# Moving one subtraction of the stick-breaking attention from the vector engine to GpSimd, and computing its scores with two stacked products instead of three

## What is computed

```
z = einsum('bqhd,bkhd->bhqk', qb, kb) * scale
mask = s_idx[None, :] < t_idx[:, None]
log_fail = where(mask, log_sigmoid(-z), 0.0)
after = cumsum(log_fail, axis=3, reverse=True) - log_fail
log_a = log_sigmoid(z) + after
a = where(mask, exp(log_a), 0.0)
out = einsum('bhqk,bkhd->bqhd', a, vb)
```

## Time and profile before

| | |
|---|---|
| times of three runs | 2904.34, 2911.0, 2911.57 us |
| the profiled execution: its own time | 2908.29 us |
| its span, from first to last instruction | 2906.5 us |
| PE busy | 2839.6 us (98%), 12826 instructions |
| DVE busy | 1793.6 us (62%) |
| ACT busy | 1019.7 us (35%) |
| POOL busy | 1006.3 us (35%) |
| TensorE clock granted, mean | 0.994 of full |
| stick stage, first to last score product | 189.7 to 365.0 us |

### The profile page before, as it was taken

The page is one execution under the profiler, slowest core; times in us unless marked ns, Lnnn a source line. Parts: engine busy times, 40 slices in busy tenths (PEclk is TensorE's granted clock), DMA queues, the critical chain, the costliest instruction groups (busy, mean ns, idle before and its releaser), DMA issues. The chain is left out here.

```text
span 2906.5 us, 32794 instructions
## 1 busy us (share of the span) xinstructions
PE 2839.6 (98%) x12826; PEld 2250.9 (77%) x12826; DVE 1793.6 (62%) x1884; ACT 1019.7 (35%) x1492; POOL 1006.3 (35%) x595
## 2 busy tenths in 40 slices
PE   8999999999999999999999999999999899999998
PEld 7876677787878888778888866776887778888876
DVE  4649954877765555883332175565538787777557
ACT  3148943566530101441002143334015455552012
POOL 2320023265543332243333330300344545553334
PEclk9999999999999999999999999999999999999999
DMA  3131032355662322321323343431341222214232
GB/s 122 51 80 30 1 138 96 136 187 206 230 217 87 116 87 95 117 103 51 116 73 129 108 113 126 109 73 48 136 150 51 87 87 80 87 74 151 88 114 88
DMA packets 111042, 308.12 MB, mean 106 GB/s; under 512 B 21744, under 2 KB 31216, under 8 KB 110128
## 3 DMA queue, kind: packets, MB, share of 16 engines
q1 hardware_dynamic: 105168, 285.40, 29.1%
q10 hardware_dynamic: 5728, 20.74, 1.8%
HBM read 212.96 MB, written 64.75 MB: 96 GB/s over the span
## 5 line engine op out<-in xcount | busy, mean ns | idle before, releaser
L327 POOL TENSOR_SCALAR w_hi<-w_raw 128x1024 fp32r<-128x1024 f32 x116 | 127.0, 1095 | 1185.3 <-PE ps L1905 229.8
L329 POOL TENSOR_TENSOR w_lo<-w_raw,w_hi 128x1024 fp32r<-128x1024 f32 x116 | 304.3, 2623 | 9.7
L420 PE MATMUL ps<-x_hi,w_hi 128*128 128x512 f32 x656 | 203.8, 392 | 0.1
L420 PE MATMUL ps<-x_lo,w_hi 128*128 128x512 f32 x656 | 202.1, 389 | 0.0
L420 PE MATMUL ps<-x_hi,w_lo 128*128 128x512 f32 x656 | 201.9, 389 | 0.0
L2036 DVE TENSOR_TENSOR down_sums<-down_sums,ps 128x1024 f32<-128x1024 f32 x112 | 132.7, 1217 | 68.2 <-PE ps L1905 68.2
L3783 POOL TENSOR_TENSOR op_low<-op_sum,op_high 128x512 fp32r<-128x512 f32 x84 | 111.1, 1334 | 150.4 <-DVE op_sum L3777 104.3
L1905 PE MATMUL ps<-hidden_hi,w_hi 128*128 128x512 f32 x480 | 147.9, 389 | 2.1 <-DVE down_sums L2036 2.1
L1905 PE MATMUL ps<-hidden_lo,w_hi 128*128 128x512 f32 x480 | 147.8, 389 | 0.0
L1905 PE MATMUL ps<-hidden_hi,w_lo 128*128 128x512 f32 x480 | 147.8, 389 | 0.0
L420 PEld LDWEIGHTS ps<-x_hi,w_hi 128*128 128x128 f32 x656 | 122.7, 188 | 27.3 <-issue 1.9
(11 more groups left out here) (573 smaller groups left out, 7603.2 us busy)
## 6 DMA issues: line engine op xcount, KB each, us to landing
w_raw<-wall SPq DMA_DIRECT2D x140, 512.0 KB, 3.8
ada_raw<-wada SPq DMA_DIRECT2D x48, 512.0 KB, 5.5
pair_raw<-wall SPq DMA_DIRECT2D x44, 512.0 KB, 4.1
hidden_scratch<-up_out SPq DMA_DIRECT2D x32, 512.0 KB, 9.0
hidden<-hidden_scratch SPq DMA_DIRECT2D x32, 512.0 KB, 4.5
up_raw<-wall SPq DMA_DIRECT2D x28, 512.0 KB, 6.9
residual<-residual_scratch SPq DMA_DIRECT2D x24, 512.0 KB, 7.1
hidden_scratch<-conv_out SPq DMA_DIRECT2D x22, 512.0 KB, 2.6
```

The costliest lines, as they stand in the source:

```text
L327: nc.gpsimd.tensor_scalar(w_hi[:, slot, :], w_raw[:, slot, :], 1.0, 1.0, ALU.mult, ALU.mult).then_inc(w_split, 1)
L329: nc.gpsimd.tensor_tensor(w_lo[:, slot, :], w_raw[:, slot, :], w_hi[:, slot, :].bitcast(F32), ALU.subtract).then_inc(w_split, 1)
L420: last = nc.tensor.matmul(ps[:, banks + c, :], lhs, x[:, k0 + k, c * HALF:(c + 1) * HALF], start=k == 0 and n == 0, stop=k == nk - 1 and n ...
```

## The change

Four things change together.

1. `low` moves from DVE to POOL, into `stick_gpsimd`, one per step. `softplus` now also waits for the low part of three steps before (the ring `stick_sp` has three places), and `low` for the two sums of four steps before.
2. Scores in two passes' worth of columns: the low keys times the high queries for both heads at once (as before, the third product), and then for each head by itself one product over 128 rows, whose upper 64 rows are the high queries and whose lower 64 rows the low queries of that head (`q_twice`), against the head's high keys written twice (`k_twice`). Columns per wide step: 512 + 256 + 256 instead of 3 x 512; in a narrow one 256 + 128 + 128 instead of 3 x 256.
3. SP copies for that: `spread_q` issues 6 DMAs a pair instead of 4, the new `double_k` 4 more, `clear_q` 2 instead of 4. DVE zeroes one tile in place of two.
4. The written order: scores and exp run one step further ahead (i+4), ln, softplus and high too (i+3). On PE `sum_later` works on step i (it was i+1) and comes before `sum_block`. On ACT the exp now stands ahead of the copy, and the probability of a narrow step comes one iteration earlier.

```diff
@@ spread_q, double_k (SP)
-        for src, dst in zip((q1_hi, q1_lo), q_wide[p % 2]):
-            for h in range(2):
-                r = slice(h * HD, (h + 1) * HD)
-                sp.dma_start(dst[r, :, h, :].bitcast(F32), src[r, p, :].bitcast(F32).rearrange("q (c n) -> q c n", c=4)
-                             ).then_inc(q_spread.sem, 16)
+        for h in range(2):
+            r = slice(h * HD, (h + 1) * HD)
+            for src, dst, to in ((q1_hi, q_wide, h), (q1_hi, q_twice, 0), (q1_lo, q_twice, 1)):
+                sp.dma_start(dst[p % 2][to * HD:(to + 1) * HD, :, h, :].bitcast(F32),
+                             src[r, p, :].bitcast(F32).rearrange("q (c n) -> q c n", c=4)).then_inc(q_spread.sem, 16)
+
+    def double_k(sp, p):
+        for h in range(2):
+            for n in range(2):
+                sp.dma_start(k_twice[p][h][n * HD:(n + 1) * HD, :].bitcast(F32),
+                             k1_hi[h * HD:(h + 1) * HD, p, :].bitcast(F32)).then_inc(q_spread.sem, 16)
...
@@ front_sync (SP)
             if b == 16:
-                sp.wait_ge(*q_zeroed.at(2))
+                sp.wait_ge(*q_zeroed.at(1))
                 spread_q(sp, 0)
+            if b == 18:
+                sp.wait_ge(w_used, 14 + 3)
+                double_k(sp, 0)
...
@@ stick_gpsimd (POOL)
-        pool.wait_ge(*spl_done.at(NS))
+        def low(k):
+            pool.wait_ge(*sph_done.at(k + 1))
+            if k >= 4:
+                pool.wait_ge(*c_full.at(k - 3))
+                pool.wait_ge(*t_done.at(sums_to(k - 4)))
+            nc.gpsimd.tensor_tensor(at(spl, k), at(sp_buf, k), at(sph, k).bitcast(F32), ALU.subtract
+                                    ).then_inc(spl_done.sem, 1)
+
+        for k in range(NS):
+            low(k)
         split_blocks(pool, GO + 1, GO + 2)
...
@@ stick_scalar (ACT)
-        for i in range(-3, NS + 1):
-            if 2 <= i + 2 < NS:
-                stick_log(act, i + 2)
-            if i >= 1:
+        for i in range(-4, NS + 1):
+            if 2 <= i + 3 < NS:
+                stick_log(act, i + 3)
+            if i >= 1 and not first_of_chunk(i - 1):
                 probability(i - 1)
+            if 0 <= i < NS and first_of_chunk(i):
+                probability(i)
+            if 2 <= i + 4 < NS:
+                stick_exp(act, i + 4)
             if 0 <= i < NS:
                 copy_later(i)
-            if 2 <= i + 3 < NS:
-                stick_exp(act, i + 3)
...
@@ stick_vector (DVE)
             dve.wait_ge(*l_done.at(k + 1))
+            dve.wait_ge(*spl_done.at(k - 2))
...
-        def low(k):
-            dve.wait_ge(*sph_done.at(k + 1))
-            nc.vector.tensor_tensor(at(spl, k), at(sp_buf, k), at(sph, k).bitcast(F32), ALU.subtract
-                                    ).then_inc(spl_done.sem, 1)
...
-        for i in range(-2, NS + 3):
+        for i in range(-3, NS + 3):
             if 0 <= i < NS:
                 add_later(i)
-            if 0 <= i + 2 < NS:
-                softplus(i + 2)
-                high(i + 2)
-                low(i + 2)
+            if 0 <= i + 3 < NS:
+                softplus(i + 3)
+                high(i + 3)
...
@@ stick_scores (PE)
-        for n, (a, b) in enumerate(((k1_hi, q_hi2), (k1_hi, q_lo2), (k1_lo, q_hi2))):
-            last = nc.tensor.matmul(z_bank(k)[:, :, columns(k)], a[:, p, ks], b[:, c, :, columns(k)],
-                                    start=n == 0, stop=n == 2, skip_group_check=True)
...
+        last = nc.tensor.matmul(z_bank(k)[:, :, columns(k)], k1_lo[:, p, ks], q_wide[p % 2][:, c, :, columns(k)],
+                                start=True, stop=False, skip_group_check=True)
...
+        for h in range(2):
+            last = nc.tensor.matmul(z_bank(k)[:, h, columns(k)], k_twice[p][h][:, ks],
+                                    q_twice[p % 2][:, c, h, columns(k)], start=False, stop=h == 1, skip_group_check=True)
...
@@ stick_tensor (PE)
-        for i in range(-3, NS + 2):
-            if 2 <= i + 3 < NS:
-                stick_scores(pe, i + 3)
+        for i in range(-4, NS + 2):
+            if 2 <= i + 4 < NS:
+                stick_scores(pe, i + 4)
+            if 0 <= i < NS:
+                sum_later(i)
             if 0 <= i + 1 < NS:
                 sum_block(i + 1)
...
-            if 0 <= i + 1 < NS:
-                sum_later(i + 1)
```

More of the change, by code:

```diff
@@ L659, in _program @@
     k1_hi, k1_lo = slots("stick_k_hi", 36, 4, F32R), slots("stick_k_lo", 28, 4, F32R)
-    q_wide = [tuple(slots(f"stick_q_{part}_{n}", first + 2 * i, 2, F32R, [P, 4, 2, STICK_Q])
-                    for i, part in enumerate(("hi", "lo"))) for n, first in enumerate((32, 12))]
+    q_wide = [slots(f"stick_q_wide_{n}", first, 2, F32R, [P, 4, 2, STICK_Q]) for n, first in enumerate((32, 12))]
+    q_twice = [slots(f"stick_q_both_{n}", first, 2, F32R, [P, 4, 2, STICK_Q]) for n, first in enumerate((34, 14))]
+    k_36 = slots("stick_k_twice_36", 36, 1, F32R)[:, 0, :]
+    k_twice = [(temp("stick_k_twice_t", 4, 1, F32R)[:, 0, :], slots("stick_k_twice_11", 11, 1, F32R)[:, 0, :]),
+               (k_36, slots("stick_k_twice_24", 24, 1, F32R)[:, 0, :]),
+               (slots("stick_k_twice_37", 37, 1, F32R)[:, 0, :], slots("stick_k_twice_25", 25, 1, F32R)[:, 0, :]),
+               (slots("stick_k_twice_38", 38, 1, F32R)[:, 0, :], k_36)]
     y_pool = slots("pool_out", 20, 4)
@@ L941, in front_vector @@
         dve.wait_ge(w_used, 12 + 3)
-        for t in q_wide[0]:
-            nc.vector.memset(t[:, :, :, :].bitcast(F32), 0.0).then_inc(q_zeroed.sem, 1)
+        nc.vector.memset(q_wide[0][:, :, :, :].bitcast(F32), 0.0).then_inc(q_zeroed.sem, 1)
     FRONT = ((square_ready, 8), (square_added, 8), (stat_full, 2), (rstd_ready, 4),
@@ L957, in _program @@
     t_sb = stick_ring("stick_later", 3, 7)
-    a_buf = stick_ring("stick_a", 4, 12)
-    sph = stick_ring("stick_sp_hi", 4, 16, F32R)
-    spl = stick_ring("stick_sp_lo", 4, 20, F32R)
+    sph = stick_ring("stick_sp_hi", 4, 10, F32R)
+    a_buf = stick_ring("stick_a", 4, 14)
+    spl = stick_ring("stick_sp_lo", 4, 18, F32R)
     o1 = slots("stick_o", 16, 4)
@@ L1006, in clear_q @@
     def clear_q(sp):
[L1008 to L1011, removed]
+        for h in range(2):
+            r = slice((1 - h) * HD, (2 - h) * HD)
+            sp.dma_start(q_wide[1][r, :, h, :].bitcast(F32), q_wide[0][r, :, h, :].bitcast(F32)).then_inc(q_cleared.sem, 16)
     def stick_sync(sp):
@@ L1018, in stick_sync @@
                 sp.wait_ge(*z_full.at(last_of_pair(p - 2)))
-                sp.wait_ge(*q_spread.at(64 * p))
+            sp.wait_ge(*q_spread.at(160 * p))
             spread_q(sp, p)
+            double_k(sp, p)
         load_blocks(sp, GO + 3, GO + 4)
-        sp.wait_ge(*q_spread.at(256))
+        sp.wait_ge(*q_spread.at(640))
     def stick_gpsimd(pool):
-        pool.wait_ge(*spl_done.at(NS))
+        def low(k):
[7 more added lines that the diff above has]
+            low(k)
         split_blocks(pool, GO + 1, GO + 2)
@@ L1088, in high @@
             dve.wait_ge(*sp_done.at(k + 1))
[L1089 to L1093, removed]
+            if k >= 5:
+                dve.wait_ge(*c_full.at(k - 4))
+                dve.wait_ge(*t_done.at(sums_to(k - 5)))
             nc.vector.tensor_copy(at(sph, k), at(sp_buf, k)).then_inc(sph_done.sem, 1)
-        def low(k):
-            dve.wait_ge(*sph_done.at(k + 1))
-            nc.vector.tensor_tensor(at(spl, k), at(sp_buf, k), at(sph, k).bitcast(F32), ALU.subtract
-                                    ).then_inc(spl_done.sem, 1)
         def add_later(k):
@@ L1149, in stick_scores @@
         pe.wait_ge(*freed(k - Z_RING))
-        for n, (a, b) in enumerate(((k1_hi, q_hi2), (k1_hi, q_lo2), (k1_lo, q_hi2))):
-            last = nc.tensor.matmul(z_bank(k)[:, :, columns(k)], a[:, p, ks], b[:, c, :, columns(k)],
-                                    start=n == 0, stop=n == 2, skip_group_check=True)
[L1153 to L1157, removed]
+        last = nc.tensor.matmul(z_bank(k)[:, :, columns(k)], k1_lo[:, p, ks], q_wide[p % 2][:, c, :, columns(k)],
+                                start=True, stop=False, skip_group_check=True)
+        if j >= 2 * c:
+            cs = columns(k).start
+            nc.tensor.matmul(z_bank(k)[:, :, cs:cs + P], ident[:, :],
+                             mask[:, :].unsqueeze(1).to_broadcast([P, 2, P]),
+                             start=False, stop=False, skip_group_check=True)
+        for h in range(2):
+            last = nc.tensor.matmul(z_bank(k)[:, h, columns(k)], k_twice[p][h][:, ks],
+                                    q_twice[p % 2][:, c, h, columns(k)], start=False, stop=h == 1, skip_group_check=True)
         last.then_inc(z_full.sem, 1)
```

11 lines of the change are left out of this document (5 added, 6 removed).

## The result

| | before | after |
|---|---|---|
| median (lowest to highest), us | 2909.64 (2904.34 to 2911.57) | 2885.86 (2884.17 to 2888.35) |
| profiled execution, us | 2908.29 | 2884.95 |
| span, us | 2906.5 | 2883.2 |
| stick stage, first exp behind the front stage to last probability, us | 175.3 | 155.3 |

The ratio is 0.9921, 95% interval 0.9907 to 0.9934: 23 us less (19 to 27). Between the two profiled executions the span fell by 23.3 us, and the stage gave 20.0 of them. In what follows "stage" is always this stretch, read from the one profiled execution of a kernel.

The account below looks back on a forecast made before the run. DVE was taken as the bound; afterwards ACT's 146 us, about 1.3 at the end and 9 of waits make a 156.3 us stage, a gain of 19, so 2891 us in all, range 2882 to 2905.

Parts of the forecast that it names:

- The bound before is DVE: Stick stage: DVE, busy 169.6 of 176 us, makes the others wait; moving the low part takes 44.6 us off it.
- The sum: Stick stage: ACT's 146 us, about 1.3 at the end and 9 of waits make 156.3, a gain of 19.
- GpSimd at 1.3 us: Low part on POOL: 1.3 us per instruction, one a step, so POOL idles at 2.0 us a step.
- Scores: Score products on PE: 0.22 us saved per wide step, 64 times, 14 us; narrow steps taken as 0.
- PE level with ACT: Middle of the stick stage: PE within 1% of ACT, 4.00 against 4.04 us for two wide steps.
- The copy between exp and ln: ACT's turn: a copy between exp and its ln saves 0.14 us per pair, 79 pairs, 11.1 us, less 2.2.
- The DMAs: SP copies for the stage: 10 a set instead of 4, there in time; cost 0, or 4 us if late.
- The last score product: Sign in the profile after: PE's last score product of the stage near 347 us in place of 365.0.
- The lock: DVE's rounding can't start while POOL works: 1.83 us loop, no loss; POOL at 1.69 gives about 2902 us; chance 0.10.
- The slower rival: Rounding and POOL's low part loop, POOL at 2.28 us: stage 205, total 2941; decides from 1.9 us; chance 0.07.
- the order: Stick stage: running one step further ahead covers POOL's low part; ACT's copies follow `sum_later` with 0.0 to 0.6 us spare.
- no change: Stick stage: a step's chain over five banks, not engine load, sets the pace; time within 9 us; chance 0.07.

Follow-up runs that it names:

- GpSimd longer: Changed kernel with GpSimd computing the first half of each wide low part twice, an additional 128x256 subtraction with its own wait: stage 165.3 us, ratio 0.9961.

## Why the prediction was right, point by point

- *The bound before is DVE; relieve it and the gain comes.* Shown: with the low part on DVE the stage is 174.4, 0.9 us shorter than before.
- *The sum, 156.3 us of stage, a gain of 19, 2889 to 2892 in all (2891 said, range 2882 to 2905).* Measured 155.3, 20.0 and 2885.86. Inside the stage two terms were off and cancelled in part: ACT was busy 148.3 us where 146 stood, and idle 7.0 where 9 of waits and 1.3 at the end stood. On the profiled execution, 2889.3 was forecast and 2884.95 measured, 4.3 us less: 1.0 in the stage; 1.2 ahead of it, which is scatter (the first exp is at 189.6 to 191.0 us in all profiles, and differs as much between kernels with the same front stage); and 2.1 behind it, where I had said that all is shifted as a whole. 1.2 of these 2.1 lie right behind the stage. GpSimd's weight split ran at 371.03 to 373.40 beside DVE's first y_lo subtraction before, which took 3.23 us; after, it ran at 348.60 to 350.98 and ended 0.9 us after DVE had begun, so that this one took 1.98. The other three took 1.21 in both. This is read from two traces, not tested; the remaining 0.9 is less than two executions differ by in the later stages.
- *GpSimd at 1.3 us.* 1.27 to 1.31 in every wide step. The slower rows came from the last MLP: there all 61 of the kind with a median of 1.69 overlapped a DVE instruction that reads SBUF alone, while of the other kind the 53 that met no such instruction took 1.31 at most.
- *Scores.* 0.22 us less in a wide step, as said; 0.07 less in a narrow one, where I took 0 (bounds 0 to 0.12).
- *PE level with ACT.* Shown for PE: with 14 us more of scores PE is busy 142.6 of 144 us and the stage is 161.4. For ACT it rests on its idle time, 5.3 us of 196 to 346, and on the copy ahead of the exp, where more work on ACT lengthened the stage; the run with less on ACT brought late copies with it and settles nothing.
- *The copy between exp and ln.* 9 us expected (0.14 in 64 steps), 7.9 measured, but only 42 wide steps had the pair to lose (5.9 us); the rest is idle time and in part the clock.
- *The DMAs.* No wait for them: `double_k` was issued from 175.50 to 178.94, and in the stage no row of the waits of PE, DVE, ACT or GpSimd names SP or a DMA.
- *The last score product, said to be near 347.* It was at 340.9, mainly since the scores also run one step further ahead: from the last score product to the last probability there were 6.3 us before and 9.3 after.
- *The lock.* The rounding does stand still while GpSimd works, as the Trainium skill, "SBUF — State Buffer", section "SBUF: two separate sides", has it: ten of the 64 wide ones were lengthened, by 3 us together. That it costs nothing was right. The slower rival was to decide from 1.9 us of GpSimd work a step. At 2.1 us a step, in two instructions, the stage is still 165.3, 10 us better than before, since the rounding comes in between the two; what a single instruction of that length would do was not run.

Where the argument was weak is *the order*. The prediction said that running ahead covers GpSimd's 1.3 us and that `sum_later` and the copies have 0.0 to 0.6 us to spare, and counted some waits for it. It priced no part of the order beyond the exp and ln, and gave 0.07 to the rival "no change", dismissed because a step's latencies add up to 7 us where five banks leave 11 (to fill them they would have to be 1.6 times as long, not twice). The runs show that this sum does not decide. Each engine takes its list in order, so one early need behind one late delivery in a turn stops it. With all of the order missing the stage is 17.6 us longer, with the depth or the sequence alone 17.7 and 17.5; with the narrow probability alone put back it is 21.4 longer, with `sum_later` alone 24.6. With any of these the change would have gained 2.5 us of the stage at most or lost up to 4.6, with the profile before looking just the same.

These prices do not add up. Only the new depth is the narrow probability, `sum_later` and the copy all put back, and it costs 17.7 us where they cost 21.4, 24.6 and 7.9 one by one (with the highest estimate for the clock taken off, 16.0 where they cost 16.3, 16.1 and 4.5). A placement is good or bad only together with the others; why the three together cost no more than one was not followed up.

That the forecast held was in part luck. I had followed the new sequence for the middle of a chunk (the 0.0 to 0.6 us), but for its ends, where the narrow probability stands, not at all. Even the changed kernel is not free of this wait: PE's scores stand behind the narrow probability in 15 places for 10.5 us, in the waits above. It does not seem to cost the stage much, since ACT idled only 7.0 us in it; one turn later the same wait is 31.9 us.

## What to carry to other kernels

When a stage is bound by one engine, add up start-to-start times of every engine for one turn of the loop: the gain ends at the next of these sums, whatever the first engine is relieved of (20 us here, of 44.6 taken off DVE). Then walk through one turn of each in-order list, and at the ends of the loop too, and ask for every wait what the engine delivering it has to do before: here each of two single placements was worth as much as the whole gain, and a third a part of it. Test such placements together as well as one by one, since their costs did not add up. Moving work onto an idle engine lengthens the path it lies on (0.69 to 1.29 us); here it needed a step more of depth, and the depth brought up the next thing that frees a buffer. And look at PE's clock before a stage time is put down to the order.

## What the runs showed of the hardware

- DVE's rounding from SBUF to SBUF that began while a GpSimd subtraction ran ended only behind it, in all 23 places of the changed kernel: a narrow one 0.15 us behind (0.65 in place of 0.29). Where the rounding had begun first, it was mostly GpSimd's subtraction that grew (in the kernel with GpSimd longer, 29 of 38 took 1.34 to 1.50 in place of 1.29). A DVE instruction with one operand in PSUM was not touched (0.69 at the longest, in 192 of them beside a GpSimd busy for 88% of the time).
- The GpSimd subtraction took 1.29 us for 512 columns and 0.73 for 256; an estimate from these two is 0.17 us fixed and 2.2 ns a column.
- Two fp32r products of 128 columns with their own weights followed each other at 0.06 and 0.11 us; two of 256 take as long together as one of 512 (0.23).
- Where PE stood still in the stage, its granted clock fell in some executions. With `sum_later` late, PE had stood from 208.6 to 210.1 us and the clock was 0.50 from 210.4 to 213.8; over 336 to 356 us its mean was 0.83 (windows view). In the changed kernel, and with the whole old order, it stayed at 1.00 through the stage. With the narrow probability late it stayed at 1.00 up to 341 us, although PE stood there too. A PE that waits in the stage can lose clock on top, but not each wait does that.

```profile
336.00:356.00 20.00, 16.86 (x84) 10.98 (x84) 12.33 (x25) 16.40 (x31) 8.32 (x8) 0.83 0.01 2
```
